# Turning seven heads' outputs with transposing DMAs in place of TensorE

## What is computed

```python
proj = x @ w_in                              # x, z and o parts, 2048 columns each, and the gates
xc = silu(conv4(xm)); q, k = xc @ w_q, xc @ w_k; v = xm @ w_v      # per head
h = mlstm_chunkwise(q, k, v, gates)          # per head, 8 chunks of 128 tokens: (tokens, 256)
hn = (h - mean(h)) * rsqrt(var(h) + eps) * norm_g                  # over the head's 256 channels
hb = sigmoid(o_pre) * hn + skip * xc
branch = (hb * silu(z)) @ w_out
```

## Time and profile before

| | |
|---|---|
| median of 3 runs | 1388.66 us (1387.12 to 1392.43) |
| profiled execution, its own time | 1388.29 us |
| span of its trace | 1386.5 us |
| granted TensorE clock | 0.999 of full speed |
| busy: TensorE, VectorE, ScalarE, GpSimd | 1374.8, 1155.4, 754.4, 147.5 us |

### The profile page before, as it was taken

One profiled execution on the slowest core, in us unless ns is written; L12 is line 12 of the kernel. 1 busy time (PEld: TensorE's weight loads), 2 busy tenths in 40 slices (PEclk: granted clock), 3 DMA queues, 4 the chain that ended last, 5 costly groups with the idle time before them and its releaser, 6 DMA issues.

```text
span 1386.5 us, 19098 instructions
## 1 busy us (share of the span) xinstructions
PE 1374.8 (99%) x6602; PEld 1150.8 (83%) x6602; DVE 1155.4 (83%) x1891; ACT 754.4 (54%) x1318; POOL 147.5 (11%) x246
## 2 busy tenths in 40 slices
PE   9999999999999999999999999999999999999997
PEld 7888888888888888888888888888888888888886
DVE  6989899898998989899874446797888888889976
ACT  5775766657576674757733436564333333336340
POOL 1001011010201101010000001001111111100021
PEclk9999999999999999999999999999999999999999
DMA  6115344262534426245497767434666555699651
GB/s 235 49 39 145 97 123 112 72 182 54 140 96 118 118 76 172 65 137 180 138 334 244 221 190 226 129 118 112 168 159 165 156 135 157 180 298 324 215 198 76
DMA packets 103809, 213.44 MB, mean 154 GB/s; under 512 B 11010, under 2 KB 27906, under 8 KB 102562
## 3 DMA queue, kind: packets, MB, share of 16 engines
q1 hardware_dynamic: 90914, 178.66, 38.7%
q0 software_dynamic: 12800, 33.56, 13.0%
HBM read 170.11 MB, written 75.63 MB: 177 GB/s over the span
## 4 chain that ended last, share of the span: by engine, by line
PE 94%; DVE 3%; ACT 1%; DMA 1%; issue 1%; POOL 0%; DVEq 0%; SPq 0%; ACTq 0%; POOLq 0%
PE wide L2935 20%; PE wide L2937 20%; PE wide L2936 20%; PE ps_state L2935 3%; PE ps_state L2937 3%; PE ps_state L2936 3%; PE ps_inter L2936 2%; PE ps_inter L2935 2%; PE ps_inter L2937 2%; PE ps_intra L3114 2%; PE ps_intra L2937 2%; PE ps_intra L2935 2%; PE ps_s L2935 2%; PE ps_s L2936 2%; PE ps_s L2937 2%; PE ps_intra L2936 2%
## 5 line engine op out<-in xcount | busy, mean ns | idle before, releaser
L2936 PE MATMUL wide<-xa,inb 128*128 128x512 f32 x576 | 224.7, 390 | 0.0
L2935 PE MATMUL wide<-xb,inb 128*128 128x512 f32 x472 | 189.5, 402 | 0.7 <-DVE inb L1941 0.5
L2937 PE MATMUL wide<-xb,inb 128*128 128x512 f32 x472 | 184.3, 391 | 0.0
L2936 PEld LDWEIGHTS wide<-xa,inb 128*128 128x128 f32 x576 | 108.4, 188 | 20.2
L2936 PE MATMUL wide<-xa,blk 128*128 128x512 f32 x320 | 124.5, 389 | 0.0
L2937 PEld LDWEIGHTS wide<-xb,inb 128*128 128x128 f32 x472 | 88.6, 188 | 19.2
L2935 PEld LDWEIGHTS wide<-xb,inb 128*128 128x128 f32 x472 | 88.8, 188 | 18.5 <-issue 0.8
L2935 PE MATMUL wide<-xb,blk 128*128 128x512 f32 x256 | 99.7, 389 | 0.0
L2937 PE MATMUL wide<-xb,blk 128*128 128x512 f32 x256 | 99.6, 389 | 0.0
L1860 ACT ACTIVATE wy<-wy_raw 128x1024 fp32r<-128x1024 f32 x56 | 59.4, 1062 | 61.0 <-DMA wy_raw<-y_block 60.7
L2935 PE MATMUL wide<-xa,inb 128*128 128x512 f32 x208 | 83.2, 400 | 0.7 <-DVE inb L1941 0.7
(11 more groups left out here) (439 smaller groups left out, 3951.3 us busy)
## 6 DMA issues: line engine op xcount, KB each, us to landing
in_raw<-in_w_in SPq DMA_DIRECT2D x45, 512.0 KB, 4.2
wy_raw<-y_block SPq DMA_DIRECT2D x56, 256.0 KB, 4.2
mw_raw<-h_block SPq DMA_DIRECT2D x53, 256.0 KB, 3.3
m_sum<-in_w_out POOLq DMA_DIRECT2D x48, 256.0 KB, 4.3
h_block<-f_buf SPq DMA_DIRECT2D x48, 256.0 KB, 3.5
w_sum<-in_pool_w_out POOLq DMA_DIRECT2D x48, 256.0 KB, 4.3
a_raw<-in_pool_w_z SPq DMA_DIRECT2D x16, 512.0 KB, 3.7
a_raw<-folded SPq DMA_DIRECT2D x16, 512.0 KB, 4.6
```

The source lines that it names most:

```text
L2935: pe.matmul(dst, a[0], b[0], start=first, stop=False, skip_group_check=more)
L2936: pe.matmul(dst, a[0], b[1], start=False, stop=False, skip_group_check=more)
L2937: return pe.matmul(dst, a[1], b[0], start=False, stop=last, skip_group_check=more)
```

## The change

TensorE no longer turns heads 0 to 6. For each token half f ScalarE parts the normalised numbers into their two 16-bit halves (`part_turn`, into `apart`), SP turns each half with one transposing DMA of 128 x 1024 16-bit elements (`move_turned`, into `turned_halves`), and ScalarE joins them into float32 again (`join_turn`, into `joined`), from where VectorE's `y_turned` reads. `apart` and `joined` lie where `xm_hi`, `qT` and `kT` do, `turned_halves` where `num` does; hence the waits on `s_full` in `part_turn` and on `turn_taken` in `high_xm`. The orders of ScalarE, VectorE and SP are changed; `in_snapshot` of an o pair waits for one count of `y_sum` for each part; two semaphores are shared with later uses. The eighth head is turned as before.

```diff
...
 F32R = mybir.dt.float32r
+U16 = mybir.dt.uint16
 
...
                 xc_hi = sA("xc_hi", [P, 2, S], F32R, whole)
+            with ExitStack() as whole:
+                turned_halves = sA("turned_halves", [P, 2 * NC * (DV + 1)], U16, whole)
             num = sA("num", [P, NC, DV + 1])
...
                 xm_hi = sA("xm_hi", [P, 2, S], F32R, whole)
+            with ExitStack() as whole:
+                apart = sA("apart", [P, 2, 2, S], U16, whole)
+            with ExitStack() as whole:
+                joined = sA("joined", [P, 2, 2, HALF], F32, whole)
             qT = sA("qT", [P, S])
...
             return (w_first_in[j], 16) if p == 1 else (w_half_in[j], 16 * max(p, 1))
+
+        def turned_at(f, part):
+
+            at = f * (2 * S + PAD) + part * S
+            return turned_halves[:, at:at + S].rearrange("p (n t) -> p n t", t=P)
 
...
         hn_ready = sem("hn_ready")
+        h_apart = sem("h_apart")
+        h_moved = sem("h_moved")
         turn_full = sem("turn_full")
...
         fold_taken = sem("fold_taken")
-        x0_hi = sem("x0_hi")
+        x0_hi, X0_HI = h_apart, 2 * (HEADS - 1)
         x0_lo = sem("x0_lo")
...
         ln_done_late = sem("ln_done_late")
-        wg_in = sem("wg_in")
+        wg_in, WG_IN = h_moved, 64 * (HEADS - 1)
         wu_in = [sem(f"wu_in{r}") for r in range(WU_RING)]
...
                 sp.dma_start(qw[:, :], wi_rows[h, :].partition_broadcast(P)).then_inc(decay_in, 16)
+
+            def move_turned(h, f):
+
+                sp.wait_ge(h_apart, 2 * h + f + 1)
+                if f:
+                    sp.wait_ge(h_moved, 64 * h + 32)
+                for part in range(2):
+                    sp.dma_start_transpose(turned_at(f, part), apart[:, f, part, :]).then_inc(h_moved, 16)
 
...
                 load_in(3 * h + 1, 1)
+                move_turned(h - 1, 0)
                 load_qkv(h)
...
                 load_rows(h)
-                store_h(h - 1, 1, 2)
+                move_turned(h - 1, 1)
                 load_in(3 * h + 2, 1)
-                store_h(h - 1, 5, 3, 7)
+                store_h(h - 1, 1, 2, 5, 3, 7)
                 if h < HEADS - 1:
...
                 if h and kind == O_OF:
-                    act.wait_ge(y_sum, H_PARTS * (h - 1) + H_PART[3])
+                    act.wait_ge(y_sum, H_PARTS * (h - 1) + {1: 1, 6: 2, 5: H_PART[3]}[q])
                 act.activation(in_target(p, j, n), wide[:, p % 2, :], ACT.Copy).then_inc(in_snap, 1)
...
                 act.wait_ge(conv_ready, 2 * h + 2)
-                if h == 0:
+                if h:
+                    act.wait_ge(turn_taken, 4 * h)
+                else:
                     act.wait_ge(rows_full, 1)
...
 
+            def part_turn(h, f, part):
+
+                act.wait_ge(hn_ready, 2 * h + f + 1)
+                act.wait_ge(s_full, NC * (h + 1))
+                ins = act.activation(apart[:, f, part, :].rearrange("p (c d) -> p c d", d=DV),
+                                     num[:, 4 * f:4 * f + 4, 0:DV].bitcast(U16).rearrange("p c (d b) -> p c d b", b=2)[:, :, :, part], ACT.Copy)
+                if part:
+                    ins.then_inc(h_apart, 1)
+
+            def join_turn(h, f, part):
+
+                act.wait_ge(h_moved, 64 * h + 32 * (f + 1))
+                ins = act.activation(joined[:, f, :, :].bitcast(U16).rearrange("p j (c t b) -> p c j t b", t=P, b=2)[:, :, :, :, part],
+                                     turned_at(f, part).rearrange("p (c j) t -> p c j t", j=2), ACT.Copy)
+                if part:
+                    ins.then_inc(turn_full, 2)
+
             def gate_rows(m):
...
                 else:
-                    act.wait_ge(wg_in, 16 * (g + 1))
+                    act.wait_ge(wg_in, WG_IN + 16 * (g + 1))
                 raw, hi, _ = group_part(g, m)
...
                 take_num(h - 1, 6)
+                part_turn(h - 1, 0, 0)
+                part_turn(h - 1, 0, 1)
                 take_num(h - 1, 7)
...
                 in_high(x + 11)
-                in_high(x + 12)
                 in_snapshot(3 * h + 1, 1)
                 first_tap(h, 1)
+                in_high(x + 12)
+                norm_head(h - 1, 1)
+                part_turn(h - 1, 1, 0)
+                part_turn(h - 1, 1, 1)
                 in_high(x + 13)
-                high_qkv(h)
-                norm_head(h - 1, 1)
                 in_high(x + 14)
...
                 in_snapshot(3 * h + 1, 6)
+                join_turn(h - 1, 0, 0)
+                join_turn(h - 1, 0, 1)
                 in_upper_right(3 * h)
                 in_snapshot(3 * h + 1, 5)
+                join_turn(h - 1, 1, 0)
+                join_turn(h - 1, 1, 1)
                 in_high(x + 16)
                 in_high(x + 17)
+                high_qkv(h)
                 in_high(x + 18)
...
                 at = COL_G + 2 * h + j
-                turned = (ps_inter, ps_s)[m % 2][:, :] if b is None else b
+                turned = joined[:, n, j, :] if b is None else b
                 dve.wait_ge(turn_full, 4 * h + m + 1)
...
                 in_sum(3 * h + 1, 0)
-                y_turned(h - 1, 0)
+                chunk_stats(h - 1, 6)
                 in_sum(3 * h + 1, 1)
-                y_turned(h - 1, 1)
-                in_low(x + 10)
-                chunk_stats(h - 1, 6)
-                in_sum(3 * h + 1, 2)
-                in_sum(3 * h + 1, 3)
-                in_join(3 * h, 4)
                 chunk_stats(h - 1, 7)
                 scales(h - 1, 1)
+                in_low(x + 10)
+                in_join(3 * h, 4)
+                in_sum(3 * h + 1, 2)
+                norm_scale(h - 1, 1)
+                in_sum(3 * h + 1, 3)
                 in_low(x + 11)
                 in_join(3 * h + 1, 2)
-                y_finish(h - 1, 0)
-                norm_scale(h - 1, 1)
+                in_low(x + 12)
                 tap(h, 1, 1)
-                in_low(x + 12)
-                y_finish(h - 1, 1)
                 in_low(x + 13)
...
                 in_low(x + 15)
-                y_turned(h - 1, 2)
-                y_finish(h - 1, 2)
 
...
                 tap(h, 1, 3)
+                y_turned(h - 1, 0)
+                in_join(3 * h + 1, 5)
+                y_turned(h - 1, 1)
                 in_sum(3 * h + 2, 0)
-                y_turned(h - 1, 3)
-                in_join(3 * h + 1, 5)
                 in_low(x + 16)
...
                 in_sum(3 * h + 2, 2)
+                y_turned(h - 1, 2)
+                y_finish(h - 1, 0)
+                y_turned(h - 1, 3)
+                in_join(3 * h + 1, 4)
+                y_finish(h - 1, 1)
+                y_finish(h - 1, 2)
+                in_low(x + 18)
                 h_difference(h - 1, 5)
+                in_sum(3 * h + 2, 3)
                 y_finish(h - 1, 3)
-                in_join(3 * h + 1, 4)
-                in_sum(3 * h + 2, 3)
+                tap(h, 0, 1)
                 h_difference(h - 1, 7)
                 h_difference(h - 1, 6)
-                tap(h, 0, 1)
-                in_low(x + 18)
                 in_low(x + 19)
...
             def first_half_lo(n):
-                dve.wait_ge(x0_hi, n + 1)
+                dve.wait_ge(x0_hi, X0_HI + n + 1)
                 at = (B11, B21)[n // 4]
...
 
-            def turn_head(h, m):
-
-                if m == 1:
-                    pe.wait_ge(s_taken, NC * (h + 1))
-                elif m:
-                    pe.wait_ge(turn_taken, 4 * h + m - 1)
-                turn(h, m, (ps_inter, ps_s)[m % 2])
-
             pe.wait_ge(const_set, 2)
...
                     gate_columns()
-                if h:
-                    if (kind, q) == (X_OF, 5):
-                        turn_head(h - 1, 0)
-                    elif (kind, q) == (Z_OF, 1):
-                        turn_head(h - 1, 1)
-                    elif (kind, q) == (Z_OF, 6):
-                        turn_head(h - 1, 2)
-                    elif (kind, q) == (Z_OF, 7):
-                        turn_head(h - 1, 3)
                 if (kind, q) == (O_OF, 5):
...
                     query_or_key(h, 0, [wide[:, (h + 1) % 2, :], wide[:, 2, :]],
```

## The result

The changed kernel takes 1411.8 us (median of 4 runs, 1411.18 to 1412.92) where the kernel before took 1388.23 on the same chip: a ratio of 1.0168, 95% interval 1.0148 to 1.0188, so +23.6 us. The profiled execution took 1411.18 us, its span is 1409.4. The forecast was 1401 within 1388 to 1435.

What follows compares the result with a forecast made beforehand. TensorE's stream was taken as the bound, VectorE as second with 0.4 us to spare. Per head, 3.6 us late at the values less 1.76 saved gave +1.8, +12.7 over seven: 1401 us, own range 1395.7 to 1410, wide range 1388 to 1435.

Steps and rivals of the forecast that it cites:

- The bound: TensorE's stream bounds the kernel; VectorE is a second bound from (z,5) to the values, 0.4 us to spare in 19.1.
- The removed turns: TensorE loses four turns of 0.44 us in each of seven heads: 1.76 us per head, 12.3 in all.
- ScalarE's copies: Eight parting and joining copies per head on ScalarE, 0.95 us each (bounds 0.5 and 1.9), 7.6 us per head.
- The transposes: Four 256 KB transposing transfers per head on SP's queue cost nothing, covered by 12.6 and 7.3 us of room.
- rival D: Transposing transfers go tile after tile, a pair taking 23 us: +200 us, about 1600 (about 1575 by another estimate); chance 0.04.
- The count on VectorE: From in_join(z,5) to low_qkv VectorE has 22 operations instead of 15, 20.6 us instead of 16.4: +0.6 us per head.
- stall (a): Behind snapshot (z,5) ScalarE's two joins delay high part x+16, so VectorE waits 0.6 us.
- Stall (b): tanh_z(1) waits for block 5's later store, so VectorE gets high part x+19 late: 0.6 us, up to 1.4.
- +1.8 us per head: TensorE is 3.6 us late at the values, less 1.76 saved; over seven heads +12.7 us.
- A: VectorE keeps up and TensorE takes only its shorter stream, 12.3 us less: 1376.4; chance 0.10.
- B: Only VectorE's count binds, both further stalls are hidden: +4.5 us, 1393; chance 0.17.
- C: The second transposed pair lands late, in 11.6 us, and shifts ScalarE and VectorE by 4.3 per head: +30, 1431; chance 0.14.

Runs made afterwards that it cites:

- e1: The changed kernel with ScalarE's high parts for (o,7) and (o,5) moved ahead of tanh_z(1), which waits for block 5's store: 1403.47 us.
- e8: e1 with one VectorE tap of 1.28 us per head, tap(h, 0, 1), left out in heads 1 to 7: 1395.31 us.
- e4: The kernel before, with one transpose instead of four in each turn of heads 0 to 6: 1383.04 us, ratio 0.9967.
- e10: Half of the change: only each head's first pair goes by transposing DMA, TensorE turns the second as before: 1385.52 us, ratio 0.9978 to the kernel before.
- e2: The changed kernel with its 28 transposing DMAs replaced by plain copies of the same bytes, the turning left out: 1409.99 us.
- e3: The changed kernel with 20 idle transposes of the identity on TensorE ahead of (o,7) in heads 1 to 7: 1410.04 us.
- e7: e5 mended: low parts x+14, x+15 back ahead of the taps, the weight load ahead of the transposes, further ScalarE and VectorE reordering: 1392.86 us.
- e11: e9 with its moves of skip_term(1) and h_difference(4) taken back: 1394.17 us, ratio 1.0035.
- e5: The changed kernel reordered: first joins ahead of the second normalising, y_turned 0 and 1 and their sums ahead of (z,5), low_qkv sooner: 1410.68 us.
- e9: e7 with four moves against its remaining waits: a parting, skip_term(1), sum 0 of o and h_difference(4): 1398.82 us.
- e6: e1 with VectorE's low parts x+19 and x+20 moved ahead of tap (0,1) and of differences 7 and 6: 1414.91 us.

## Why the prediction was right, and which term was mis-sized

**The bound.** Right: TensorE's stream gave way to VectorE between snapshot (z,5) and low_qkv. e1 shows the stretch at 22.2 us in all seven heads, whatever TensorE's clock does in it, and e8 takes 1.2 us off it with one tap of 1.28. e4 says less than I had asked of it: its waits go back to a weight load.

**The removed turns.** 112 matmuls are gone as counted. 1.76 us per head were predicted. From the values to the next snapshot (z,5) the kernel before takes 63.3 us, the changed one 61.5 to 61.6, so 1.7 to 1.9 less; e4 is 1.3 shorter for three quarters (1.32), e10 0.7 to 0.9 for a half (0.88). The 0.44 us a turn are right.

**ScalarE's copies.** Taken at 0.95. The partings take it (two in 1.99). The joins take 1.36 us each, two in 2.58, within my bounds of 0.5 and 1.9, but 0.34 above the value taken; that is per copy, 0.7 per pair on the way to high part x+16.

**The transposes.** Costed at nothing behind 12.6 and 7.3 us of room: right in the changed kernel (4.5 us median; e2). "SP waits for nothing new that matters" held, nearly: the load of (o,0) went out behind the second pair at 384.64, 0.6 us after its buffer was free at 384.06, and VectorE did not wait for it in this head. "At their old times, or a tenth later" was too good for the load ahead of it: it went out at 375.74, 49.6 us behind the last values where the kernel before has 48.9, landed 6.3 us later instead of 4.0, and ScalarE waited 1.2 us for it. A whole transfer of 128 x 1024 16-bit elements took 4.5 us where e2's plain copy took 3.0, both medians. The Trainium skill, "Advanced Engine Details and Errata", section X-Bar Transpose (TRN2), has transposing DMAs as fast as regular ones; here they took half as long again, and the measurement decides. The estimate of 10.5 us a transfer, from the 1309 ns a tile of the Trainium skill, "VectorE: DVE Perf Modes", section The three transpose paths, is far above the 4.5, and rival D with it.

**The count on VectorE.** 22 operations, 20.6 us predicted. From the end of snapshot (z,5), 387.64, to low_qkv's end, 410.31, are 22.7 us; predicted were 397.9 − 376.06 = 21.8 with the stalls, so 0.8 to 0.9 more in this head. y_turned from SBUF takes 0.66 back to back, the same as from PSUM in the earlier trace rows, not 0.60 (+0.2 in four); in_join starts 0.2 later, behind a y_turned; stall (a), put at 0.6, is 0.81 of idle time, for high part x+16 is ready 0.5 us later behind the snapshot than predicted (the longer joins) and VectorE comes to it 0.3 later. The 1.7 us of idle time that I had put ahead of in_join were not there. In this head low part x+14 waited 1.1 us for its weights and two taps took 3.31 us instead of 2.60 (last section); five of the seven heads have idle time there at all, 0.3 to 0.8 us.

**Stall (b), the store.** The step itself is right, and mis-sized. Difference 5 was to end at 385.8 − 376.06 = 9.7 us behind the snapshot and ended 10.6 behind it, and tanh_z(1) waited 3.44 us (4 predicted). But in heads 3 and 5 the store takes 4.1 and 3.9 us to land, not 2.1 or 2.85. In head 3 a GpSimd transfer was issued 1 us ahead of it (310.86 and 311.91 us), in head 5 1.9 us ahead; but in head 1 one went out 1.8 us ahead of a store that landed in 2.4. So I suspect these transfers, and no run shows it. In heads 3 and 5 the stall is 4.6 and 4.4 us instead of 2.5 to 2.8.

**The sum.** The step that was mis-sized is "+1.8 us per head", 12.7 in all; from the first head's values to the last's the changed kernel takes 23.3 us more. In the head shown it is 2.8, in the two with the late store 4.7 and 4.6: (410.44 − 326.10) − (396.06 − 314.52) = 2.8, and (326.10 − 239.80) − (314.52 − 232.93) = 4.7. Of the 1.0 that is missing in the first, 0.8 is the chain just told, and 0.1 lies between the end of low_qkv and the first value matmul (410.31 and 410.44). In head 1 another 1.0 is a wait of TensorE behind a snapshot that I had not listed. Three terms were too small, all the same way: the joins, y_turned's length, and the store's landing. The clock's fall was not on my list at all; that it cost next to nothing here (e3) is luck. 1411.8 us, nearly twice the forecast's loss, lies just above the forecast's own range (1395.7 to 1410); the wide range held it only because its upper end was put there for late transposes, which did not come.

**What I placed wrongly.** I had the larger stall at the values and 1.7 us at (o,7). It came out as 2.5 at (o,7) and then none at the values in six heads, because the clock's fall made the products between last 1.7 us longer. Only in the seventh head, where the clock held, does the wait for qkv show (1.39 us). e3 shows both in one picture.

**The rivals.** A (1376) needed VectorE to be through from the snapshot to low_qkv in 18.2 us; it took 22.7 in the head shown and 22.2 in e1. B (1393, the count alone) put that at 20.6; with the store's wait gone ahead of (o,7) e1 still has 22.2, of which stall (a) is some 0.9, and takes 1403.5. Another order (e7, e11) comes to B's time, not the one that B was about. C and D needed late transposes; they landed in 4.5 us, 7.2 at most, and e2 excludes them.

**What stays open.** Why e7 and e11 stay at 1393 where I expected 1381: their waits sum to 13 to 16 us over those of before, so it is the same bound in part, and in e11 VectorE waits 7 us for weights besides. I found no order of the whole change that clears it, and can't say that none exists. The waits, clock and turns account for e7's span up to 3 us, and for e11's up to 3.5; that rest I haven't placed.

## What to carry to other kernels

Ahead of moving work off the busiest engine, count the second engine's work between two fixed points, here a snapshot that can't start sooner and the operand that TensorE needs next: with 0.4 us to spare in 19, seven operations moved into it cost more than all the matmuls saved. Move only the half that has slack in front of the fixed point (e10), and when a wait is taken away, look up every engine's next one, loads whose buffer comes free later and stores among them: the expectations of e5, e7, e9 and e11 failed there. And before a wait is called a sign that the second engine is full, look at what that engine itself waited for: in e4 it was a load of weights.

A stall's price is not its length. Behind six of seven stalls of 2.5 us and more TensorE ran at half its clock for 3.4 us; that is nearly free where the next operand is late anyway (e3) and costs about 2 us a time where it isn't (e6: 11.9 us in six heads).

## What the runs showed of the hardware that I had not expected

- The clock falls behind a short idle time. In the changed kernel it fell behind six stalls of 2.5 to 4.6 us and held behind one of 2.53; in e1 it fell behind three of seven stalls that are alike (1.94 to 2.04); in e9 behind one of 2.14 and not behind one of 2.22; in e8, with stalls up to 1.98, never; in e3 once, at 7.7 us behind a wait of 1.95, and not in the heads. It stayed at 0.50 for 3.4 us each time, and once, in e6 behind 3.89 us, for 6.8. The stall's length alone does not decide it.
- A 16-bit copy is not as fast as its count of elements says when it is the output that is strided: 1.36 us written with a stride of two (joins), 1.05 us read with one (partings), both of 1024 elements. Two f32 copies of this length take 2.01.
- A transposing DMA holds SP's queue longer: its issue takes 1.3 us in the median, 1.2 to 4.5, where e2's plain copies of the same bytes take 0.5 to 0.6.
- VectorE slows down beside one GpSimd instruction. Two taps took 3.31 us where two take 2.60 without it:

```profile
383.97 3.31 DVE L2044 SCALAR_TENSOR_TENSOR xx<-xx,cols 128x1024 f32<-128x1024 f32 x2
```

```profile
384.86 1.35 POOL L1129 TENSOR_SCALAR_AFFINE_SELECT m_bc<-m_bc 128x1024 f32<-128x1024 f32 x1 [9.14 <-DMA qw<-wi_rows]
```

In the kernel before one low part took 1.58 us instead of 0.69 at 370.31, and the same GpSimd instruction ran there from 370.05. I made no run that moves it away, so the cause is argued, not shown.
